# The second block's position bias moved from reversing matmuls on TensorE to an add on VectorE

## What is computed

```python
def dilated_window_attention(q, k, v, bias_table, window, dilation):
    ...
    rel = qi + W - kj
    valid = (rel >= 0)[None] & (rel <= W)[None] & (key_pos >= 0)
    bias = bias_table[t5_causal_bucket(jnp.clip(rel, 0, W) * dilation)]
    bias = jnp.transpose(bias, (2, 0, 1)).astype(jnp.float32)[:, None]
    s = jnp.einsum('bdhnqe,bdhnke->bdhnqk', qb, kb).astype(jnp.float32) * (E ** -0.5) + bias
    s = jnp.where(valid, s, NEG_INF)
    lse = jax.nn.logsumexp(s, axis=-1)
    p = jnp.exp(s - lse[..., None])
    o = jnp.einsum('bdhnqk,bdhnke->bdhnqe', p.astype(v.dtype), vb)
```

## Time and profile before

| | |
|---|---|
| median of 3 runs | 1575.58 us (1574.8 to 1578.62) |
| the profiled execution: its time | 1577.1 us |
| its span, first to last instruction | 1575.3 us |
| mean granted TensorE clock | 0.97 of 2.4 GHz |
| TensorE matmuls busy | 1489.3 us (95%) |
| VectorE, ScalarE, GpSimd busy | 692.7 us (44%), 543.9 us (35%), 443.7 us (28%) |
| the attention of the second block | 883.7 to 924.8 us of the span, 2.6% of it |

### The profile page before, as it was taken

One profiled execution on the slowest core, in us unless ns is written; L12 is line 12 of the kernel. 1 busy time (PEld: TensorE's weight loads), 2 busy tenths in 40 slices (PEclk: granted clock), 3 DMA queues, 4 the chain that ended last, 5 costly groups with the idle time before them and its releaser, 6 DMA issues.

```text
span 1575.3 us, 21537 instructions
## 1 busy us (share of the span) xinstructions
PE 1489.3 (95%) x8270; PEld 1087.3 (69%) x8270; DVE 692.7 (44%) x1070; ACT 543.9 (35%) x816; POOL 443.7 (28%) x160
## 2 busy tenths in 40 slices
PE   7989999998989999999979989999899999999997
PEld 6778899987778899987766768974445435444442
DVE  3785465564775475554316625553221111212111
ACT  5546543344646533335434431112111111111111
POOL 3372343434362444437886311100000000000000
PEclk9999999999989999999998979999999999999999
DMA  6442355554332355556763601026599999999995
GB/s 235 141 133 76 108 188 194 180 197 146 121 133 76 134 174 201 180 195 195 235 203 111 227 5 55 1 107 290 215 419 427 429 428 428 425 422 422 428 427 226
DMA packets 44426, 351.91 MB, mean 223 GB/s; under 512 B 5187, under 2 KB 7151, under 8 KB 19759
## 3 DMA queue, kind: packets, MB, share of 16 engines
q1 hardware_dynamic: 43646, 349.37, 58.0%
q10 hardware_dynamic: 576, 1.13, 0.2%
q0 software_dynamic: 112, 0.17, 0.1%
HBM read 347.71 MB, written 1.07 MB: 221 GB/s over the span
## 4 chain that ended last, share of the span: by engine, by line
PE 71%; DVE 8%; DMA 8%; issue 6%; DVEq 2%; ACT 2%; POOL 1%; POOLq 0%; SPq 0%; ACTq 0%
PE psum L1032 13%; PE psum L1033 12%; PE psum L1034 12%; PE psum L1652 12%; DMA ring<-in_w_expert_up 7%; PE psum L1679 5%; PE psum L1021 3%; PE psum L1611 3%; PE psum L1620 1%; PE psum L1100 1%; PE psum L1484 1%; DVE arena L2163 1%; DVE arena L2206 1%; DVE stat L2216 1%; PE psum L1119 1%
## 5 line engine op out<-in xcount | busy, mean ns | idle before, releaser
L878 POOL TENSOR_TENSOR weights_split<-weights_raw,weights_split 128x2048 fp32r<-128x2048 f32 (+4 forms) x108 | 389.6, 3620 | 428.8 <-ACT weights_split L1753 428.7
L1753 ACT ACTIVATE weights_split<-weights_raw 128x2048 fp32r<-128x2048 f32 (+4 forms) x154 | 243.3, 1584 | 283.3 <-PE psum L1034 283.0
L1652 PE MATMUL psum<-ring,arena 128*64 128x512 f32 x976 | 229.2, 604 | 11.2 <-DMA ring<-in_w_expert_up 10.1
L1652 PEld LDWEIGHTS psum<-ring,arena 128*64 128x64 f32 x976 | 74.4, 139 | 148.7 <-issue 148.7
L1032 PE MATMUL psum<-weights_split,h_split 128*128 128x512 f32 (+3 forms) x400 | 154.9, 387 | 15.8 <-DVE arena L2440 6.4
L1033 PE MATMUL psum<-weights_split,h_split 128*128 128x512 f32 (+3 forms) x400 | 153.0, 382 | 0.0
L1034 PE MATMUL psum<-weights_split,h_split 128*128 128x512 f32 (+3 forms) x400 | 152.7, 382 | 0.0
L1032 PE MATMUL psum<-weights_split,hidden_split 128*128 128x512 f32 (+1 forms) x384 | 151.6, 395 | 0.0
L1033 PE MATMUL psum<-weights_split,hidden_split 128*128 128x512 f32 (+1 forms) x384 | 150.1, 391 | 0.0
L1034 PE MATMUL psum<-weights_split,hidden_split 128*128 128x512 f32 (+1 forms) x384 | 149.7, 390 | 0.0
L1032 PE MATMUL psum<-h_split,weights_split 128*128 128x256 f32 x512 | 145.2, 284 | 1.4 <-DVE weights_split L878 1.4
(11 more groups left out here) (371 smaller groups left out, 2185.7 us busy)
## 6 DMA issues: line engine op xcount, KB each, us to landing
weights_raw<-in_layer_w SPq DMA_DIRECT2D x94, 1024.0 KB, 4.8
arena<-in_w_expert_down SPq DMA_DIRECT2D x32, 2048.0 KB, 13.3
ring<-in_w_expert_up SPq DMA_DIRECT2D x32, 2048.0 KB, 16.8
ring<-in_w_expert_gate SPq DMA_DIRECT2D x29, 2048.0 KB, 16.1
weights_raw<-in_second_w SPq DMA_DIRECT2D x44, 512.0 KB, 4.2
arena<-in_w_expert_gate SPq DMA_DIRECT2D x3, 2048.0 KB, 9.1
weights_raw<-in_layer_w SPq DMA_DIRECT2D x6, 768.0 KB, 4.1
ring<-in_w_out SPq DMA_DIRECT2D x2, 2048.0 KB, 17.1
```

Source lines behind the costliest of these rows:

```text
L878: eng.tensor_tensor(W.part(j, 1, n), W.raw(j, n), W.part(j, 0, n).bitcast(F32), ALU.subtract).then_inc(W.lo[W.pieces[j][1]], 1)
L1652: ins = pe.matmul(bank[half(j), :], xe[h][:, k, half(j)], w[j][:, k, :], start=(k == 0), stop=(k == KD - 1))
L1753: act.activation(W.part(j, 0, w), W.raw(j, w), ACT.Copy).then_inc(W.hi, 1)
```

## The change

Four edits belong together. The queries are turned reversed: for the query banks of `qkT`, the transposes against `ident` become matmuls against `flip`, so rows of the scores come out reversed, like `bias_m`. The reversing matmuls of `bias_m` are gone. VectorE adds `bias_m` to the scores while it moves them from PSUM to `att_s[i % 2]`; that empties the banks, so plan and `emptied_by` name "V", and since `att_s[i % 2]` is written earlier in the loop now, VectorE first waits for PT(i - 2). Maximum and exponential read `att_s`, in place, and ScalarE's tiny copy is gone. Last, the output rows are reversed too, so `attT` turns them back by matmuls against `flip`. The wait for the load of `bias_m` moves from TensorE to VectorE.

```diff
--- before.py
+++ after.py
@@ -375,7 +375,7 @@
     plan += interleave("qkT", 6, (4, 5, 6, 7), "A")
     for i in range(NA + 2):
         if i < NA:
-            plan.append(("S", i, ((0, 1), (2, 3))[i % 2], "A"))
+            plan.append(("S", i, ((0, 1), (2, 3))[i % 2], "V"))
         if 1 <= i <= NA:
             plan.append(("PT", i - 1, (4, 5), "A"))
         if i >= 2:
@@ -1371,14 +1371,17 @@
                 units.finish(("lora", 3 * t + 2), pe.matmul(bank, loraT[rest, 2, c], lora_w[rest, 2, :], start=False, stop=True))
             project("gate", GATE_BLOCKS)
 
-            pe.wait_ge(bias_loaded, 16)
             pe.wait_ge(qk_ready, 1)
             for j in range(6):
                 bank = units.begin(("qkT", j))
                 for c in range(2):
                     for t in range(T):
                         col = j // 3 * ATT_W + (2 * (j % 3) + c) * P
-                        ins = pe.transpose(bank[:, c * SEQ + t * P:c * SEQ + (t + 1) * P], qkv[:, t, col:col + P], ident)
+                        o = bank[:, c * SEQ + t * P:c * SEQ + (t + 1) * P]
+                        if j < 3:
+                            ins = pe.matmul(o, qkv[:, t, col:col + P], second("flip"), start=True, stop=True)
+                        else:
+                            ins = pe.transpose(o, qkv[:, t, col:col + P], ident)
                 units.finish(("qkT", j), ins)
             units.wait_emptied(*(("qkT", j) for j in range(6)))
             for i in range(NA + 2):
@@ -1386,15 +1389,9 @@
                     t, hg = ATT_UNITS[i]
                     bank, nk = units.begin(("S", i)), (t + 1) * P
                     r = slice(ATT_E * (hg % 2), ATT_E * (hg % 2 + 1))
-                    per_bank = 512 // SEQ if t else GRP
-                    for g0 in range(0, GRP, per_bank):
-                        g1 = min(g0 + per_bank, GRP)
-                        pe.matmul(bank[:, g0 * nk:g1 * nk].rearrange("p (g k) -> p g k", k=nk), second("flip"),
-                                  bias_m[:, g0 * HPG + hg:(g1 - 1) * HPG + hg + 1:HPG, SEQ - nk:SEQ], start=True, stop=False)
-                        for g in range(g0, g1):
-                            c = (g * HPG + hg) // 2
-                            ins = pe.matmul(bank[:, g * nk:(g + 1) * nk], qT[r, c, t * P:(t + 1) * P], kT[r, c, 0:nk],
-                                            start=False, stop=(g == g1 - 1))
+                    for g in range(GRP):
+                        c = (g * HPG + hg) // 2
+                        ins = pe.matmul(bank[:, g * nk:(g + 1) * nk], qT[r, c, t * P:(t + 1) * P], kT[r, c, 0:nk], start=True, stop=True)
                     units.finish(("S", i), ins)
                 if 1 <= i <= NA:
                     t = ATT_UNITS[i - 1][0]
@@ -1437,7 +1434,8 @@
             bank = units.begin(("attT", 0))
             for k in range(2):
                 for t in range(T):
-                    ins = pe.transpose(bank[:, k * SEQ + t * P:k * SEQ + (t + 1) * P], att[:, t, k * P:(k + 1) * P], ident)
+                    ins = pe.matmul(bank[:, k * SEQ + t * P:k * SEQ + (t + 1) * P], att[:, t, k * P:(k + 1) * P], second("flip"),
+                                    start=True, stop=True)
             units.finish(("attT", 0), ins)
             w = weights(("att_out", 0))
             units.wait_emptied(("attT", 0))
@@ -1973,10 +1971,9 @@
                 if i < NA:
                     n = GRP * (ATT_UNITS[i][0] + 1) * P
                     act.wait_ge(att_max, i + 1)
-                    act.activation(att_s[i % 2][:, 0:n], units.wait_full(("S", i))[:, 0:n], ACT.Exp,
+                    act.activation(att_s[i % 2][:, 0:n], att_s[i % 2][:, 0:n], ACT.Exp,
                                    bias=rowmax[:, i % 2:i % 2 + 1], accum_out=rowsum[:, i % 2:i % 2 + 1])
                     act.drain()
-                    units.emptied_by(("S", i), act.activation(stat[:, 91:92], stat[:, 91:92], ACT.Copy), "A")
                     act.sem_inc(att_exp, 1)
                 if i >= 1:
                     n = GRP * (ATT_UNITS[i - 1][0] + 1) * P
@@ -2505,12 +2502,20 @@
             dve.drain()
             dve.sem_inc(preproc_done, 1)
 
+            dve.wait_ge(bias_loaded, 16)
             for i in range(NA + 2):
                 if i < NA:
                     t, hg = ATT_UNITS[i]
                     nk = (t + 1) * P
                     m = rowmax[:, i % 2:i % 2 + 1]
-                    dve.tensor_reduce(m, units.wait_full(("S", i))[:, 0:GRP * nk], AX.X, ALU.max)
+                    biased = att_s[i % 2][:, 0:GRP * nk]
+                    if i >= 2:
+                        units.wait_full(("PT", i - 2))
+                    bank = units.wait_full(("S", i))[:, 0:GRP * nk].rearrange("p (g k) -> p g k", k=nk)
+                    units.emptied_by(("S", i), dve.tensor_tensor(
+                        biased.rearrange("p (g k) -> p g k", k=nk), bank, bias_m[:, hg::HPG, SEQ - nk:SEQ], add), "V")
+                    dve.drain()
+                    dve.tensor_reduce(m, biased, AX.X, ALU.max)
                     dve.drain()
                     dve.tensor_scalar(m, m, -1.0, None, mul).then_inc(att_max, 1)
                 if 1 <= i <= NA:
```

## The result

| | before | after |
|---|---|---|
| median of 20 runs each | 1575.84 us | 1584.12 us |
| lowest and highest | 1567.63 to 1578.62 | 1575.93 to 1597.65 |
| profiled execution | 1577.1 us, span 1575.3, mean clock 0.970 | 1582.92 us, span 1581.1, mean clock 0.963 |
| attention, first `qkT` matmul to first matmul of the `cum` line | 40.9 us | 48.6 us |

The change makes the kernel slower by 0.68% (ratio 1.0068, 95% interval 1.0047 to 1.009). The forecast was 1583.6 us.

The account below looks back on a forecast made before the run. TensorE was taken to bound the loop. At half clock the loop ends 7.1 us later, line 1422 adds 0.4 and `attT` 0.45: +8.0; 1577.1 + 8.0 - 1.5 = 1583.6 us, range 1574 to 1589.

Parts of the forecast that it names:

- I expect the fall there: Start of the attention loop: emptier for some 6 us, so TensorE's clock falls to half; forecast branch, chance 0.79.
- It doesn't come back within the loop: Rest of the attention loop: half clock stays at 0.50 from about 890 to 930 us; the loop ends 7.1 us later.
- S(0): First unit's scores: start at about 888.6 us instead of 887.5, 1.1 us later (bounds 0.6 and 1.35).
- PT(0): First unit's transposes: start at 891.8 us, with 40.1 us from there to the end of the last values at half clock.
- The add: VectorE's bias add after each unit's scores: 0.56 and 0.96 us, bounds 0.4 and 1.2; costs nothing at half clock.
- L1419: Eight instructions behind the loop (line 1422 before): 6.8 us all at half clock instead of 5.99, counted as +0.4.
- the other branch: Attention loop if the clock stays up: units of 2.4 and 4.0 us, bound by the chain through VectorE and ScalarE.
- rival 1: Attention loop: the clock stays up, the loop ends 5.3 to 6.5 us early, total 1570 us; chance 0.12.
- the flips in the start: Query banks of `qkT`: reversing matmuls cost TensorE 1.35 us more, partly hidden by ScalarE's copies, leaving 1.1 us.
- rival 3: Attention loop: the clock falls and TensorE slows 2.2 times instead of twice, 45.5 instead of 38.7 us, total 1590; chance 0.03.
- the densest part: Bias matmuls in the loop: among the wide 128-row work said to raise the clock, gone with the change.
- The rule against it: Skill page on the clock: only idle gaps longer than any here bring falls, so the clock would stay up.

Follow-up runs that it names:

- e1: Kernel before without its reversing bias matmuls and nothing in their place (bias and mask left out): 1594.98 us against 1573.25, ratio 1.0138; attention stage 46.6 us.
- e2: Changed kernel with the bias matmuls put back, overwritten by the scores, VectorE's add kept: median 1583.99 us, ratio 1.0069; attention stage 41.6 us.
- e7: Changed kernel with unread 128 x 128 matmuls at the loop's start, in later units and at its end: 1570.53 us, ratio 0.9973 to before.
- e9: Kernel before with ScalarE copying the last `qkT` bank four more times ahead of the first scores: 1605.04 us, one run; attention stage 69.0 us.
- e5: Changed kernel with plain transposes for `qkT` and `attT` instead of matmuls against `flip`: 1586.3 us against 1575.16, ratio 1.0067; attention stage 47.2 us.
- e8: Changed kernel with unread 128 x 128 matmuls only ahead of the first scores and the first transposes: 1577.56 us, one run; attention stage 43.8 us.
- e6: Kernel before with unread 128 x 128 matmuls at the end of its attention loop alone: 1571.22 us against 1574.74, ratio 0.9974.
- e4: Changed kernel with unread matmuls of 256 columns at the start, in every later unit and at the end: 1582.62 us, ratio 1.0072 to before.

## Why the prediction was right, and where its terms were off

**The mechanism.** "I expect the fall there": it came at 892.1, and half clock held for 44.4 us against my 40. "It doesn't come back within the loop": right. e1, e2, e7 and e9 show the cause from both sides, by the stage: removal alone loses, ballast gives back, and a gap brings the old loop down.

**The terms, in the profiled execution.** S(0) at 888.68 (said: 888.6). PT(0) at 891.97 (said: 891.8). From there to the end of O(7) 40.58 us (said: 40.1). The add takes 0.56 and 0.96 us, the values taken from the neighbouring rows. The end of the loop is at 932.55 instead of 931.9. Then L1419: 5.50 us where I put 6.8. The clock rose earlier in it than even in the kernel before, which takes 1.3 off. At the end of these eight matmuls the kernel is 7.24 us late (938.05 against 930.81), and I had 7.5. At the first product of the core it is 7.4 late with `attT` in, and I had 8.0. What is left unsettled is small.

**The total hit closer than its parts.** From the profiled execution I predicted 1585.1 and took 1.5 off to come to the median. The profiled execution took 1582.92, 2.2 less: 0.6 up to the core's first product, 0.4 from there to the expert stage, 1.2 in that stage, by the half-clock stretches that before had and after had not. The median of after lies 1.2 above its profiled execution instead of 1.5 below. The two misses cancel. With runs that spread from 1575.93 to 1597.65 that closeness is luck; the 7 to 8 us of the stage are not.

**Two terms off in the other branch.** For full clock I gave periods of 2.4 and 4.0 us. e7 had 2.67 and 4.29 (with 0.86 of ballast in each), and at the one place where the chain through VectorE and ScalarE is bare it took 4.35 us (912.55 to 916.90) against my 4.3. So the chain of rival 1 was sized rightly, its periods weren't measured without ballast, and its total of 1570 needed ballast that no one had put in. And I left the flips in the start at 1.1 us of the path; by e5 they cost 1.4 in the stage, the upper bound I gave. The ratio of 2.2 in rival 3 was that of the last unit alone: within the loop at half clock twelve value products took 2.45 to 2.47 us, 1.9 times the 1.29.

**One reason in it was wrong.** I wrote that what raised the clock was gone with the bias matmuls, "the densest part". e9 has them all and its clock doesn't rise for 68 us either. In these runs the bias matmuls held the clock (e2) and did not bring it back (e9). The forecast didn't hang on it, as both give 0.50 to the end, but the picture did: the loss isn't that the new loop recovers worse, it is that it goes to the lower level at its start (or at 906.8 us, in e8) and the old one doesn't.

**The rule against it.** The Trainium skill, "TensorE: Matmul & The Clock Gate", section "Why this matters for your kernels", lays falls of the clock in the middle of a kernel to idle gaps between bursts that are longer than the one ahead of PT(0). In the change TensorE is idle for 2.03 us, from the end of S(1) at 889.94 to PT(0) at 891.97, and the clock fell behind it; in e1, from 890 to 892 us, it was busy for 0.63. So the trace goes on disagreeing, and a gap shorter than the page's was dear. Gaps as the page describes them stand in the traces too, 3.75 us ahead of S(0) in e9 and 3.27 us ahead of L1430 in the kernel after (939.73 to 943.00), and the clock fell there as well. On transposes the same page, section "Part 4: PE-mode transpose", is contradicted once more by the kernel after. At 943.3 us the clock had fallen again, and from there to 948 us TensorE ran only L1430, fp32 transposes. Under them it rose:

```profile
945.00:946.00 1.00, 1.00 (x6) 1.00 (x5) 0.69 (x1) 0.74 (x2) 0.00 (x0) 0.50 0.00 0
946.00:947.00 1.00, 1.00 (x8) 1.00 (x7) 0.00 (x0) 0.74 (x2) 0.62 (x1) 0.64 0.07 16
947.00:948.00 1.00, 1.00 (x11) 1.00 (x10) 0.00 (x0) 0.96 (x3) 1.00 (x2) 1.00 0.00 0
```

**What stays open.** Why e2 has a median 11 us above its profiled run, whose loop held the clock; where four of the 20 runs of after, at 1595.7 to 1597.7 us, lost their time (their clock of 0.953 to 0.956 is that of e1, whose second fall is in the core, but no such run was profiled); and what decides whether the core falls near 985 to 995 us, since the same stretch is followed by a fall in some traces and not in others. Ballast there wasn't tried.

## What to carry to other kernels

Before taking work off a bound TensorE, look at the granted clock in the stretches around it, and ask whether what remains, above all in the fill of a pipeline, still keeps the engine as full: in e1 9.6 us less work made the stage 5.7 us longer. If a gap is unavoidable, a few small matmuls that nobody reads, sized so that they fit in it, are cheap (e6 gains 0.26% with 22 of them); ballast that exceeds the gap is a new bound (e4). And compare such kernels by stage in the trace and over many runs, since one clock fall elsewhere is larger than the effect.

## What the runs showed of the hardware that I had not expected

- A loop in which TensorE is busy all the time can run at either clock level: the old loop's stage took 40.9 us in the kernel before, most of it at 2.4 GHz, and 69.0 us, nearly all of it at 1.2 GHz, in e9 (one run), where the gap ahead of it was 2.7 us longer.
- fp32 matmuls of 128 rows and 256 columns, counted as two instructions each, took 0.235 us per instruction in e4's loop (2.35 for ten), and 128 columns 0.144 (0.87 for six, e7). In longer bursts it was less: 0.216 for 256 columns (3.89 for eighteen, e4) and 0.112 for 128 (2.01 for eighteen, e7). At half clock the mixed work of the loop slowed by 1.7 to 1.9, the scores by 1.58 / 0.86 = 1.84.
- Less work made a kernel slower by 1.4% (e1, a good part of it by the second fall in the core), and useless work made one faster by 0.26% (e6).
